# Modulation products of 128x32 column tiles: two k tiles to a batch in the opening and in blocks 23 to 38

## The reference, cut to what matters

```python
c_act  = silu(c);  cc_act = silu(c_ctx)
shift, scale, gate = split(c_act @ w_ada + b_ada, 3)       # w_ada: 2048 x 6144 per layer; cc_act likewise
h  = rmsnorm(x, norm_g) * (1 + scale) + shift              # the modulation
u  = h @ w_in                                              # combined projection: 40 blocks of 128 columns
...                                                        # convolution, RG-LRU and attention branches
x  = x + gate * (concat(branches) @ w_out)                 # 16 further blocks of 128 columns
```

## Time and profile before

| what | value |
|---|---|
| median of three runs | 1262.2 us |
| profiled execution: span from first to last instruction | 1262.1 us |
| its mean granted TensorE clock | 0.993 |
| TensorE busy | 1225.4 us, 97% |
| VectorE, ScalarE busy | 794.3 us, 543.5 us |
| opening, blocks 0 to 6 of layer 0 | TensorE from 19 us to 156 us |
| modulation products in blocks 7 to 38 (L629) | 384 matmuls from 167.7 to 633.8 us |
| modulation products in the opening (L666) | 256 matmuls from 21.0 to 139.5 us |

### The profile page before, as it was taken

How to read it: one execution, slowest core, us unless ns; L and a number is a source line. 1 busy time by engine, 2 the same in 40 slices (tenths; PEclk the granted TensorE clock), 3 DMA queues, 4 the chain that set the end, 5 groups by cost and what they waited for, 6 DMA issues and landing times.

```text
span 1262.1 us, 16910 instructions
## 1 busy us (share of the span) xinstructions
PE 1225.4 (97%) x6838; PEld 975.6 (77%) x6838; DVE 794.3 (63%) x1252; ACT 543.5 (43%) x857; POOL 9.8 (1%) x11
## 2 busy tenths in 40 slices
PE   3999999999999999999999999999999999999996
PEld 1555776666777777776778888989888988899995
DVE  5444556766756667763465555696799977656554
ACT  5222445542223433355342222355775455575542
POOL 0000100000000000000000000000000000000000
PEclk9899999999999999999999999999999999999998
DMA  9999756555764444333446666433332544325542
GB/s 335 350 348 348 228 189 232 221 201 204 266 246 167 142 142 166 129 111 142 153 165 231 221 225 225 151 134 133 136 107 101 196 144 150 119 103 205 189 167 67
DMA packets 80894, 236.36 MB, mean 187 GB/s; under 512 B 9392, under 2 KB 54192, under 8 KB 59440
## 3 DMA queue, kind: packets, MB, share of 16 engines
q1 hardware_dynamic: 80816, 235.27, 52.5%
HBM read 230.54 MB, written 2.10 MB: 184 GB/s over the span
## 4 chain that ended last, share of the span: by engine, by line
PE 94%; DMA 2%; DVE 2%; SPq 1%; ACT 1%; issue 0%; DVEq 0%; ACTq 0%
PE psum_block L789 23%; PE psum_block L790 22%; PE psum_block L791 22%; PE psum_ada L629 4%; PE psum_ada L666 2%; PE psum_scores L816 2%; PE psum_scores L717 1%; PE psum_scores L866 1%; PE psum_scores L853 1%; PE psum_scores L719 1%; PE psum_scores L718 1%; PE psum_scores L886 1%; SPq L578 1%; DMA glu<-in_w_ada 1%; DMA raw<-in_w_ada 1%; PE psum_block L913 1%
## 5 line engine op out<-in xcount | busy, mean ns | idle before, releaser
L789 PE MATMUL psum_block<-h_hi,w_hi 128*128 128x256 f32 (+1 forms) x1648 | 562.1, 341 | 0.3 <-DVE h_lo L1346 0.3
L790 PE MATMUL psum_block<-h_lo,w_hi 128*128 128x256 f32 (+1 forms) x1648 | 553.4, 336 | 0.0
L791 PE MATMUL psum_block<-h_hi,w_lo 128*128 128x256 f32 (+1 forms) x1648 | 553.2, 336 | 0.0
L1354 DVE TENSOR_TENSOR w_lo<-raw,w_hi 128x1024 fp32r<-128x1024 f32 x210 | 254.7, 1223 | 332.7 <-ACT w_hi L1006 332.4
L1006 ACT ACTIVATE w_hi<-raw 128x1024 fp32r<-128x1024 f32 x210 | 220.3, 1057 | 444.0 <-PE psum_block L791 409.5
L789 PEld LDWEIGHTS psum_block<-h_hi,w_hi 128*128 128x128 f32 x1648 | 312.7, 190 | 61.8 <-issue 26.9
L790 PEld LDWEIGHTS psum_block<-h_lo,w_hi 128*128 128x128 f32 x1648 | 312.9, 190 | 32.7 <-issue 1.9
L791 PEld LDWEIGHTS psum_block<-h_hi,w_lo 128*128 128x128 f32 x1648 | 312.8, 190 | 32.6
L1623 DVE SCALAR_TENSOR_TENSOR Y<-glu,small,Y 128x512 f32<-128x512 f32 (+1 forms) x240 | 130.4, 612 | 0.0
L1163 ACT ACTIVATE T<-psum_scores,stats 128x512 f32<-128x512 f32 (+1 forms) x48 | 29.0, 616 | 46.5 <-DVE stats L1671 46.5
L629 PE MATMUL psum_ada<-raw,cstat 128*32 128x512 f32 x384 | 47.8, 600 | 0.0
(11 more groups left out here) (212 smaller groups left out, 1193.3 us busy)
## 6 DMA issues: line engine op xcount, KB each, us to landing
raw<-in_w_blocks SPq DMA_DIRECT2D x105, 1024.0 KB, 4.9
raw<-in_w_ada SPq DMA_DIRECT2D x81, 1024.0 KB, 6.8
qreg<-in_w_blocks SPq DMA_DIRECT2D x8, 896.0 KB, 11.5
glu<-in_w_ada SPq DMA_DIRECT2D x5, 1024.0 KB, 11.6
kv<-in_w_ada SPq DMA_DIRECT2D x5, 1024.0 KB, 11.9
bd<-in_w_ada SPq DMA_DIRECT2D x5, 1024.0 KB, 11.9
Y<-in_xT SPq DMA_DIRECT2D x8, 512.0 KB, 8.1
T<-in_xT SPq DMA_DIRECT2D x16, 256.0 KB, 5.2
```

The costliest lines, as they stand in the source:

```text
L789: mm(ps[:, cols], hi, hh[:, k, t], start=(at == 0), stop=False)
L790: mm(ps[:, cols], hi, hl[:, k, t], start=False, stop=False)
L791: last = mm(ps[:, cols], lo, hh[:, k, t], start=False, stop=(at == DT - 1))
L1354: V.tensor_tensor(wl[:, u % 4, 0:n], raw_of(item)[:, cols], wh[:, u % 4, 0:n].bitcast(F32), ALU.subtract).then_inc(*C.up("lo", u))
```

## The change

`ada_plan` puts two products into every second block from 23 on (23, 25, ..., 37) and none into the blocks between. Through `stream` this moves the transfers too. `beside` puts both products of `late` after step 4 (`tp - 2`) and both of `ahead` after step 11 (`tp + 5`).

```diff
-    plan = {b: [rest.pop(0) for _ in range(2 if b < GATE1_AT - DT else 1)] for b in range(OPEN[0], GATE1_AT)}
+    single = GATE1_AT - DT
+    plan = {b: [rest.pop(0) for _ in range(2)] for b in range(OPEN[0], GATE1_AT) if b < single or (b - single) % 2 == 0}

-    steps = {(i + 1) * tp // (len(late) + 1): item for i, item in enumerate(late)}
-    steps.update({tp + 4 + i: item for i, item in enumerate(ahead)})
-    return tp, steps
+    return tp, {tp - 2: late, tp + 5: ahead}

-                            if g == 0 and step == max(s for s in steps if s < tp):
+                            if g == 0 and step == tp - 2:
                                 bridge(3)
-                            if step in steps:
-                                ada0_mm(*steps[step][1:])
+                            for item in steps.get(step, []):
+                                ada0_mm(*item[1:])
```

## The result

The changed kernel took 1264.53 us (median of 11 runs, 1263.34 to 1265.83) against 1261.91 us before (11 runs, 1261.03 to 1263.3). The ratio is 1.0020, 95% interval 1.0011 to 1.0029: 2.5 us slower (2.6 by the medians), where 0.7 us faster was forecast. The time lies in the stated range; the sign was wrong.

The account below looks back on a forecast made before the run. TensorE, busy 97% of the span, was taken to bound the kernel. The opening's -3.3, the blocks' merges -2.8 and block 35's stop +5.4 gave -0.7 us: 1261.5 us, range 1258.6 to 1265.3.

Parts of the forecast that it names:

- 1.6 us of half clock: After the stop in block 35, TensorE's clock falls to half for 3.20 us; 1.6 us lost, bounds 0 and 3.3.
- mechanism in block 35: The second product's transfer waits for the pointwise weights' slot; TensorE stands still 4.0 us, the place costs 5.4 in all.
- the part on the merges: Blocks 23 to 38: seven of eight pairs gain 0.40 us each, 2.8 in all; the cover is enough.
- the opening's: Groups 0 to 6: twelve merges worth 4.4 us, held by the transfers to a gain of about 3.3.
- the price of a merge: Two batches of one product made into one of two: 0.40 us saved in the blocks, 0.37 in the opening.
- the transfers' lead: Opening, second product of `late`: its data lands 2.7 us before use in group 4, 3.4 in group 6.
- The statement that the profile stands 0.1 us under the median: The profiled execution's span of 1262.1 us was counted against the runs' median of 1262.2.
- 2.6 us of waits on the modulation's data: TensorE's waits on the modulation's data: 2.6 us in two waits, before 50 us.
- Rival A: Block 35's stop costs more, by a later landing and longer half clock: 1265.1 us; slower past 6.1 us there; chance 0.16.

Follow-up runs that it names:

- control: The kernel before, unchanged, run for a second profile: 1262.11 us, ratio 1.0001, span 1260.0 us.
- filled: The changed kernel with 22 matmuls that nobody reads between block 35's two modulation products: 1262.63 us, ratio 1.0004 to the kernel before.
- blocks_only: The kernel before with the new plan of the blocks, the opening as before: 1266.17 us, ratio 1.0032.
- gap34: The kernel before with only block 34's modulation product moved to block 33: 1262.82 us, ratio 1.0004.
- even: The changed kernel with the pairs in blocks 24, 26, ..., 38 instead of 23, 25, ..., 37: 1257.88 us, ratio 0.9966 to the kernel before.
- half_open: open_only with 14 transfers of the opening halved, so its output is another: 1254.96 us, ratio 0.9944 to the kernel before.
- even_blocks: The kernel before with pairs in blocks 24, 26, ..., 38, the opening as before: 1259.58 us, ratio 0.9983.
- open_only: The changed kernel with the old plan of the blocks, so only the opening is changed: 1260.62 us, ratio 0.9987 to the kernel before.
- swap: The changed kernel with block 37's weights listed ahead of the pointwise weights in block 35: 1258.42 us, ratio 0.9972 to the kernel before.

## Why the prediction was wrong

By stages, from the starts in two profiles, the changed kernel against control, in us:

```
stage                                           control   changed   difference   forecast
start to block 7                                 154.12    152.22      -1.9         -3.3
block 7 to the transposes in block 35            420.96    418.90      -2.1         -2.4
to the first modulation product of block 35       14.70     15.70      +1.0          0
to block 36                                        1.00      7.00      +6.0         +5.9
block 36 to the transposes in block 37            25.90     26.08      +0.2         -0.5
to the end                                       643.32    642.90      -0.4         -0.4
sum                                             1260.0    1262.8       +2.8         -0.7
```

The forecast's 1.6 us of half clock are split here as its terms fell: 0.8 before block 36 and 0.8 behind it.

**The mechanism in block 35 was right**, and so were most of its sizes: issue with the end of L912, landing after 5.0 (4.9 forecast), a stop of 4.06 us (4.0). The clock was sized from the milder of two rows: 1.6 us, where the changed kernel lost 2.3 (0.87 in the second product, which took 1.87 us to the next matmul instead of 1.0, and 1.4 in block 36) and filled gave back 1.9. blocks_only lost 1.6, with a stop as long (3.9 us) and the clock's fall in another place. The term of 1.6 was within its bounds and 0.3 to 0.7 too small.

**The step that failed in kind** is in the part on the merges: the prediction saw that the block after the scores comes 1.2 us sooner, and judged the cover by the last of these groups alone, block 37, 4.1 us. Block 35 is the one stretch where something else hangs on the same chain, the layer norm's four tiles and the pointwise products, and there the cover was 0.4 us. That cost 1.0 us. gap34 shows it alone, even shows it gone. It could have been read before: the end of `ln_y` against the pointwise products stands in the timeline of before.

**The term that was mis-sized most** is the opening's: -3.3 forecast, -1.6 to -2.1 measured. That it would be held by its transfers was right (half_open), and the price of a merge too (0.35 against 0.37). The size was the transfers' lead, 3.4 us, and that was a figure of one long execution: in it TensorE had lost 2 us more ahead of block 7 than in control, so the transfers were further ahead of it. With control's lead of 2.1 the same working gives about -2.1. The five profiles with the old opening have a lead of 3.3 or 3.4 us in before, gap34 and even_blocks, which took 1.1 to 2.2 us more than the median of their kernel, and of 2.1 and 1.8 in control and blocks_only, which took 0.3 and 1.4 less. So the typical lead lies near control's. The statement that the profile stands 0.1 us under the median was where this began: a span leaves out 1.8 us of an execution's time. (The 2.6 us of waits on the modulation's data leave out another 1.9 us, on `glu` at 30.8 us; nothing hangs on it.)

In sum: -0.7 forecast, +1.2 to +1.7 for the opening, +1.0 for the pointwise products, +0.3 to +0.7 for the clock, +0.3 for merges worth 0.35 instead of 0.40 in the blocks: +2.1 to +3.0, measured +2.5. Rival A (the stop costs more than 6.1 us) is not what tipped the sign: the clock's excess of 0.3 to 0.7 and the stop's of 0.1 would by themselves have brought the sum to between -0.3 and +0.1, no change that can be seen.

Before and control differ by run-to-run scatter of the opening: block 7 started at 156.3, 154.1, 153.3, 155.7 and 156.4 us in five profiles with the old opening (before, control, blocks_only, gap34, even_blocks), and at 152.2, 153.0, 153.5, 152.0 and 152.8 in five with the new (changed kernel, open_only, swap, even, filled). In the longest of them (156.3 and 156.4) the issue at about 40 us took 5.0 to 5.2 us; in control it took 4.5, in blocks_only 3.6. It took 3.6 in gap34 too, with block 7 at 155.7, and 5.0 in filled, at 152.8, so it doesn't explain the scatter by itself. Why is open. Less what each execution took above the median of its kernel, the starts are 154.2 to 154.7 with the old opening and 152.2 to 153.0 with the new, about 1.9 us apart.

## What to carry to other kernels

A batch moved in a ring of slots must be checked against what holds its slot before it, here the item three places earlier: if that item is used just before the batch, the transfer starts only when its data is wanted. Cover has to be read at every repetition of a pattern, not at the last or the typical one. And a lead or a slack taken from one profile is that execution's; compare its own time, not its span, with the median first, or take a second profile.

## What the runs showed of the hardware

- Going from full matmuls to 128x32 column tiles and back costs 0.34 us each time at full clock; where no transfer is waited for, a merge gave 0.35 (14.91 against 14.21 us a group of two merges).
- A stop of about 4 us (4.06 and 3.91) brought the clock down at different points: 2.1 us into the stop in the changed kernel (then 4.8 us of work at half), and 1.2 us after work had resumed in blocks_only (3.4 us of work at half). With 22 matmuls of 384 columns in the stop it stayed at full.
- A transfer of 1 MB with nothing before it landed in 4.7 to 5.0 us in the rows shown; in the opening's full queue, where five transfers take 14.57 us, one leaves every 2.9 us.
